# When the choices of experts are made between the gathered rows: shorter steps, other units, later copies

## What is computed

```python
def peer(h, p):
    n = h.shape[0]
    q = (h @ p['peer_wq']).reshape(n, PEER_HEADS, 2, PEER_HALF)
    s = jnp.einsum('nhcd,chkd->nhck', q, p['peer_keys'], preferred_element_type=F32)
    s1, i1 = lax.top_k(s[:, :, 0], PEER_TOPK)
    s2, i2 = lax.top_k(s[:, :, 1], PEER_TOPK)
    cand_s = (s1[..., :, None] + s2[..., None, :]).reshape(n, PEER_HEADS, PEER_TOPK * PEER_TOPK)
    cand_i = (i1[..., :, None] * PEER_N_KEYS + i2[..., None, :]).reshape(n, PEER_HEADS, PEER_TOPK * PEER_TOPK)
    top_s, pos = lax.top_k(cand_s, PEER_TOPK)
    eidx = jnp.take_along_axis(cand_i, pos, axis=-1)
    g = jax.nn.softmax(top_s, axis=-1)
    act = jax.nn.gelu(jnp.einsum('nd,nhkd->nhk', h, p['peer_u'][eidx], preferred_element_type=F32))
    return jnp.einsum('nhk,nhkd->nd', (g * act).astype(h.dtype), p['peer_v'][eidx])
```

## Time and profile before

| | us |
|---|---|
| median of 3 runs | 1500.54 (1499.4 to 1501.41) |
| the profiled execution, its own time | 1503.75 |
| span of that execution, first to last instruction | 1502.1 |
| first gather of the experts, from the span's start | 791.95 |
| last dot | 1494.1 |

### The profile page before, as it was taken

One profiled execution on the slowest core, in us unless ns is written; L12 is line 12 of the kernel. 1 busy time (PEld: TensorE's weight loads), 2 busy tenths in 40 slices (PEclk: granted clock), 3 DMA queues, 4 the chain that ended last, 5 costly groups with the idle time before them and its releaser, 6 DMA issues. The chain is left out here.

```text
span 1502.1 us, 17250 instructions
## 1 busy us (share of the span) xinstructions
PE 1253.6 (83%) x4972; PEld 773.6 (52%) x4972; DVE 868.0 (58%) x2346; ACT 582.1 (39%) x1551; POOL 421.0 (28%) x504
## 2 busy tenths in 40 slices
PE   5998899998776977789989988877887776788786
PEld 4886588776654655578867544322332222232231
DVE  1044379997282436651135876889756895454443
ACT  1162238878373324500014443433343332343333
POOL 1320012222021300000003434434543486343331
PEclk8999899999698987989999999999999999999999
DMA  4462133324387720154139999999999987999997
GB/s 157 169 218 99 43 114 119 105 99 137 141 295 259 249 75 1 40 199 182 57 126 371 420 376 371 384 420 421 421 422 421 421 362 307 421 420 422 421 421 314
DMA packets 77881, 391.26 MB, mean 260 GB/s; under 512 B 13176, under 2 KB 22936, under 8 KB 40416
## 3 DMA queue, kind: packets, MB, share of 16 engines
q0 software_dynamic: 43104, 287.92, 47.1%
q1 hardware_dynamic: 33712, 100.68, 18.8%
q10 hardware_dynamic: 976, 1.61, 0.3%
HBM read 378.43 MB, written 11.60 MB: 260 GB/s over the span
## 5 line engine op out<-in xcount | busy, mean ns | idle before, releaser
L1963 DVE CUSTOM_DVE_ANT_0 pe_uv<-pe_uv,pe_hnat 128x1024 f32<-128x1024 f32 x264 | 321.7, 1220 | 183.5 <-DMA pe_uv<-d_uv,pe_idx 169.7
L1832 POOL DMA_INDIRECT pe_uv<-d_uv,pe_idx x256 | 309.4, 1209 | 375.5 <-PE pe_acc L1711 182.4
L1711 PE MATMUL pe_ph<-pe_uv,pe_dg 128*128 128x512 f32 x512 | 256.4, 627 | 76.7 <-ACT pe_dg L1778 76.6
L1711 PE MATMUL pe_acc<-pe_uv,pe_dg 128*128 128x512 f32 (+1 forms) x544 | 260.7, 619 | 55.6 <-ACT pe_dg L1778 55.4
L181 PE MATMUL pi_ps<-xn,pi_w 128*128 128x264 f32 x944 | 225.0, 395 | 9.5 <-PEq L87 9.5
L1711 PEld LDWEIGHTS pe_ph<-pe_uv,pe_dg 128*128 128x128 f32 x512 | 89.1, 192 | 243.4 <-ACT pe_dg L1778 176.7
L1711 PEld LDWEIGHTS pe_acc<-pe_uv,pe_dg 128*128 128x128 f32 (+1 forms) x544 | 96.7, 189 | 211.2 <-ACT pe_dg L1778 120.3
L181 PEld LDWEIGHTS pi_ps<-xn,pi_w 128*128 128x128 f32 x944 | 181.1, 195 | 41.6 <-issue 11.4
L1772 ACT ACTIVATE pe_gl<-pe_a 128x1 f32<-128x1 f32 x264 | 53.0, 201 | 345.7 <-DVE pe_a L1963 345.6
L1778 ACT ACTIVATE pe_dg<-cst,pe_w 128x128 f32<-128x128 f32 x256 | 102.7, 401 | 8.3
L1775 ACT ACTIVATE pe_w<-pe_gl,pe_gw 128x1 f32<-128x1 f32 x256 | 75.4, 295 | 8.3
(11 more groups left out here) (290 smaller groups left out, 1704.9 us busy)
## 6 DMA issues: line engine op xcount, KB each, us to landing
pi_w<-d_w_in SPq DMA_DIRECT2D x71, 512.0 KB, 3.5
mg_w<-d_w_ab SPq DMA_DIRECT2D x8, 1536.0 KB, 6.5
ss_h<-d_state SPq DMA_DIRECT2D x8, 1024.0 KB, 6.4
o_ssm_s<-ss_h SPq DMA_DIRECT2D x8, 1024.0 KB, 7.8
pq_w<-d_wq SPq DMA_DIRECT2D x16, 512.0 KB, 7.9
paged<-d_ck POOLq DMA_DIRECT2D x40, 128.0 KB, 3.3
lg_w<-d_w_in SPq DMA_DIRECT2D x10, 512.0 KB, 6.4
paged<-d_cv POOLq DMA_DIRECT2D x32, 128.0 KB, 4.8
```

The lines of the kernel that those rows point to most:

```text
L1711: mm = pe.matmul(accs[n][0:m, 4 * half:4 * half + 4, :], lhsT, uv[:, r, D_MODEL + half * 512:D_MODEL + (half + 1) * 512], start=False, sto ...
L1832: pool.indirect_dma_start(uv[:, r, :], None, k.d_uv[:], bass.IndirectOffsetOnAxis(ap=src, axis=0)).then_inc(gathered[r], 16)
L1963: dve.tensor_tensor_reduce(uv[:, r, 0:D_MODEL], uv[:, r, 0:D_MODEL], hnat[:, n, :], 1.0, 0.0, ALU.mult, ALU.add, a[:, r:r + 1]).then_inc(d ...
```

## The change

- `SPANS`: a stretch now gives the first unit and the unit at which the choice must be ready: (0, 7), (8, 22), (28, 44), (48, 64), (66, 116) and (128, 236), where they ended at 8, 24, 40, 56, 112 and 192.
- `STEPS` in place of `PACE`: the samples' choice makes one step each second unit.
- The long instructions of the comparison, multiplication and sum are cut to 4 heads each, so a choice of 8 heads has 12 of 1024 columns in place of 6 of 2048. Choices of 1 or 2 heads keep theirs, and the sums of L1899 stay whole.
- `LAG`: `weights` comes three units after `ready`. ScalarE's `exponents` comes behind the `weigh` of unit `ready`, and its wait for `chosen` stands at the first unit that uses the choice (`FIRST_USE`).
- TensorE's scores come four units after the second query, and ScalarE copies queries and scores two units after TensorE's unit.

```diff
-        SPANS = ((0, RING), (RING, 3 * RING), (3 * RING, 5 * RING), (5 * RING, 7 * RING), (7 * RING, 14 * RING),
-                 (PER, PER + 8 * RING))
-        PACE = (2, 1, 1, 1, 1, 1)
+        SPANS = ((0, 7), (8, 22), (28, 44), (48, 64), (66, 116), (PER, 2 * PER - 20))
+        STEPS = (2, 1, 1, 1, 1, 0.5)
+        LAG = 3
+        FIRST_USE = [tile * PER + h0 * TOPK for tile, h0, _ in CHOICES]
...
-        scores_at = {u + 2: n // 2 for u, n in query_at.items() if n % 2}
+        scores_at = {u + 4: n // 2 for u, n in query_at.items() if n % 2}
...
                 for i in range(LOOPS[n] * RING):
-                    for c, (first, end) in enumerate(SPANS):
-                        if BEFORE[n] + i == end:
+                    at = BEFORE[n] + i
+                    if at in FIRST_USE[1:-1]:
+                        act.wait_ge(chosen, FIRST_USE.index(at) + 1)
+                    weigh(n, i)
+                    for c, (first, ready) in enumerate(SPANS):
+                        if at == ready:
                             exponents(c + 1)
-                            act.wait_ge(chosen, c + 2)
-                    weigh(n, i)
-                    if n == 0 and i in query_at:
-                        query(query_at[i])
-                    if n == 0 and i in scores_at:
-                        scores(scores_at[i])
+                    if n == 0 and i - 2 in query_at:
+                        query(query_at[i - 2])
+                    if n == 0 and i - 2 in scores_at:
+                        scores(scores_at[i - 2])
...
+                parts = [(a, min(a + 4, H)) for a in range(0, H, 4)]
                 for which, (f, e) in enumerate(((fa, e1), (fb, e2))):
                     settled()
-                    one(dve.tensor_tensor(eq[0:m, at], f[0:m, at].unsqueeze(2).broadcast_to([m, N, TOPK]),
-                                          k.iota[0:m].unsqueeze(1).broadcast_to([m, N, TOPK]), ALU.is_equal))
-                    yield
+                    for a, b in parts:
+                        to = slice((h0 + a) * TOPK, (h0 + b) * TOPK)
+                        one(dve.tensor_tensor(eq[0:m, to],
+                                              f[0:m, to].unsqueeze(2).broadcast_to([m, (b - a) * TOPK, TOPK]),
+                                              k.iota[0:m].unsqueeze(1).broadcast_to([m, (b - a) * TOPK, TOPK]),
+                                              ALU.is_equal))
+                        yield
...
-                    for c, (first, end) in enumerate(SPANS):
-                        if at == end:
+                    for c, (first, ready) in enumerate(SPANS):
+                        if at == ready:
                             for _ in rest:
                                 pass
+                        if at == ready + LAG:
                             weights(c + 1)
                         if at == first:
                             rest = choose(c + 1)
                     dot(n, i)
-                    for c, (first, end) in enumerate(SPANS):
-                        if first <= at < end:
-                            for _ in range(PACE[c]):
+                    for c, (first, ready) in enumerate(SPANS):
+                        if first <= at < ready:
+                            for _ in range(int((at - first + 1) * STEPS[c]) - int((at - first) * STEPS[c])):
                                 next(rest, None)
```

More of the change, by code:

```diff
@@ L1921, in choose @@
                 i4 = idf[0:m, 2 * h0:2 * h1].rearrange("p (h c) i -> p h c i", c=2)
+                parts = [(a, min(a + 4, H)) for a in range(0, H, 4)]
                 for which, (f, e) in enumerate(((fa, e1), (fb, e2))):
                     settled()
-                    one(dve.tensor_tensor(eq[0:m, at], f[0:m, at].unsqueeze(2).broadcast_to([m, N, TOPK]),
-                                          k.iota[0:m].unsqueeze(1).broadcast_to([m, N, TOPK]), ALU.is_equal))
-                    yield
-                    settled()
[L1928 to L1931, removed]
+                    for a, b in parts:
[5 more added lines that the diff above has]
+                        yield
+                    settled()
+                    for a, b in parts:
+                        to = slice((h0 + a) * TOPK, (h0 + b) * TOPK)
+                        e4 = eq[0:m, to].rearrange("p (h i) j -> p h i j", h=b - a)
+                        one(dve.tensor_tensor(e4, e4, i4[:, a:b, which, :].unsqueeze(2)
+                                              .broadcast_to([m, b - a, TOPK, TOPK]), ALU.mult))
+                        yield
                     settled()
-                    one(dve.tensor_reduce(e[0:m, at], eq[0:m, at], AX.X, ALU.add))
-                    yield
+                    for a, b in parts:
+                        to = slice((h0 + a) * TOPK, (h0 + b) * TOPK)
+                        one(dve.tensor_reduce(e[0:m, to], eq[0:m, to], AX.X, ALU.add))
+                        yield
                 settled()
```

## The result

The changed kernel takes **1480.34 us** in the median of four runs (1476.51 to 1481.99), the kernel before 1500.97 us (1499.4 to 1502.4) in runs beside it. The ratio is **0.9855, 95% interval 0.9835 to 0.9874**: some 21 us faster. 1478.0 us was predicted, with a range from 1473.5 to 1490.5.

What follows compares the result with a forecast made beforehand. The prediction took the experts to be bound by DMA at 421 GB/s, with two holes to fill. Terms of 10 and 12.5 us off the median of 1500.54 gave 1478.0 us, range 1473.5 to 1490.5.

Steps and rivals of the forecast that it cites:

- What bounds the kernel: Experts, from 792 us: DMA at 421 GB/s is the bound, except in holes at 870 to 990 and 1230 to 1270 us.
- First term: Prompt's part, 870 to 990 us: late weights and late copies fill the DMA hole, 10 us, ends 0 and 11.8.
- the chain at unit 24: ScalarE waits 5.97 us for a query, VectorE 9.25 for exponents, TensorE idles 4.51; unit 32's gather goes 7 us late.
- The deduction of 1.5 us for TensorE: Units 24 to 42: TensorE needs 25.7 us per ten units against DMA's 24.9, so it falls back 1.5 us.
- Second term: Samples' choice, 1230 to 1270 us: breaking VectorE's unbroken row ends the 20.07 us gather, 12.5 us, ends 0 and 15.5.
- The rule against it: Skill page on VectorE and GpSimd's shared ports: the lock lasts one instruction, so an unbroken row would not explain 20.07 us.
- The rival built on it: Samples' choice: the long gather has another cause and comes back, 1490.5 us, chance 0.07.
- Tile 1's choice, zero: Units 66 to 116: 44 steps in 50 units, the cut ones fitting their units; extra instructions hidden beside DMA, zero cost.
- The shut-out: Rival in tile 1's choice: 12 cut steps without a pause hold GpSimd, 20.6 us lost, 1498.6 us, chance 0.04.
- The samples' lists, zero: Lists come 47 units later; their 15.1 us through DRAM is hidden in 22.4 us, with 7 us to spare, zero cost.
- The sum, 22.5 us: Whole kernel: 10 and 12.5 us off the median of 1500.54 give 1478.0 us, chance 0.77.
- What was to show it: Signs: 415 GB/s from 1190 us, weights waiting under 1 us, no long TensorE idle, last dot near 1472 us.

Runs made afterwards that it cites:

- e1_prompt_part: The changed kernel with the samples' choice put back as before, so only the prompt's part is left; 1491.19 us, ratio 0.9934.
- e5: The changed kernel with ScalarE's query and score copies back at the queries' own unit, exponents and weights still late; 1480.73 us, ratio 0.9880.
- e6: The changed kernel with exponents, ScalarE's wait and weights at one unit again, copies still late; 1480.42 us, ratio 0.9865.
- e12: The changed kernel with the prompt's old spans and copies at once, only exponents and weights late, samples' choice still changed; 1484.61 us, ratio 0.9886.
- e10: The changed kernel with late copies and late weights both undone, so the prompt's part keeps only the new spans; 1488.45 us, ratio 0.9914.
- e9: The changed kernel with eight places for query weights in place of four, weights loaded four queries earlier; 1480.09 us, ratio 0.9861.
- e4: The changed kernel with the samples' steps uncut, still one step each second unit; 1480.54 us, ratio 0.9866.
- e3: The changed kernel with the samples' choice at one step each unit, steps still cut in two; 1482.53 us, ratio 0.9876.
- e7: The kernel before with the samples' choice run on all 128 partitions in place of 8; 1488.41 us, ratio 0.9929.
- e2: The kernel before with only the samples' choice changed: steps cut, one each second unit; 1489.35 us, ratio 0.9920.

## Why the prediction was right, step by step

- **What bounds the kernel.** Right. With both holes filled the experts run at DMA's pace, 420 to 422 GB/s in every stretch from 790 to 1390 us.
- **First term, 10 us with ends 0 and 11.8.** Measured 171.0 - 160.5 = 10.5 us from unit 8 to unit 70 (10.7 in e1_prompt_part). The mechanism was half told. I followed the chain at unit 24 and let both delays take part; e5 and e6 show that, at the new spans, either alone does it, and e12 that a second wait stands behind the chain at unit 40, for scores, which the new spans remove. The new spans, which I gave no price of their own, bring 2.1 us alone (e10). The deduction of 1.5 us for TensorE was right in kind: in the changed kernel it doesn't pause from 805.82 to 925 us, and e9 shows it as the bound as soon as there is less to transfer.
- **Second term, 12.5 us with ends 0 and 15.5.** Measured 195.6 - 184.0 = 11.6 us from unit 130 to unit 202. The size was right: the hole itself was 12.4 us, and one more late landing of another kind (last section) takes 1.0 of them back. The cause was too wide. "VectorE's unbroken row" was the observation, and a row is one of three conditions. The rest that I counted on is enough by itself (e4); that the cut steps are, too (e3), I did not foresee. The estimate of at most 4.6 us for a hold was kept: 3.32.
- **The rule against it.** The Trainium skill, "SBUF — State Buffer", section "SBUF: two separate sides", has the lock between VectorE and GpSimd held for one whole instruction, by VectorE in a two-port mode or with two inputs in SBUF. With 128 partitions the trace agrees (e7): 3.05 us beside a step of 2.29 with two inputs, 0.94 beside a sum, which has one. With 8 partitions it disagrees: 20.07 us over six steps, two of them sums, and the dots between, and in e4 no passage between a step and the dot behind it. The rival built on it fell with e1, e2 and e4.
- **Tile 1's choice, zero.** The shut-out didn't move there: gathers beside the cut steps take 1.97 to 2.00 us. The piece 70 to 130 is 1.8 us longer than before, as it is in e1_prompt_part, whose steps in it are whole; so the cut is not the reason. The last section has it: late landings beside loads of code, three in place of one.
- **The samples' lists, zero.** SyncE starts them from 1404.29 to 1410.31 us, and the piece from 202 to the end is 162.1 us long, as in e3 (161.8), whose choice ends long before.
- **The sum, 22.5 us.** The medians moved by 20.6, the ratio says 21.8. In the experts of the two profiles it is 19.6: 10.5 + 11.6 and 0.4 ahead of unit 8, less 1.8 and 1.1 in the two other pieces. The late landings of the last section are the term that I did not have.
- **What was to show it.** VectorE's waits and TensorE's idle time went as said. One stretch, 1390 to 1430 us, has 410 GB/s and not 415. The last dot starts at 1466.86 us and not near 1472: the 7.5 us ahead of the experts again.

## What to carry to other kernels

Where DMA sets the pace, look for the stretches in which it is not full, follow the late transfer to the engine that waits, and put a few units of distance into that chain; here one break in it was enough, and the second is cover. Where a gather on GpSimd is held beside VectorE, any of a pause, a shorter instruction or more partitions may free it, so try the cheapest. And compare two kernels by landings inside the stage that was changed: here one profile of each was off by 7.5 us for reasons ahead of it.

## What the runs showed of the hardware

**Few partitions hold a gather.** A whole step of 8 x 2048 and one of 128 x 2048 take the same 2.3 us, yet in an unbroken row GpSimd gets through at the end of the second and not of the first.

**Beside loads of program code, gathers land a microsecond late.** Units land 2.484 us apart in the median of the pieces 70 to 130 and 130 to 202 of the changed kernel, but eight of them (73, 86, 103, 133, 136, 155, 177 and 201) land 3.4 to 3.5 us behind the one ahead; outside these pieces units 54 and 240 do too. On VectorE's timeline such a unit is unit 54, whose dot waits 1.62 us where the one ahead waits 0.19:

```profile
933.47 1.23 DVE L1975 CUSTOM_DVE_ANT_0 pe_uv<-pe_uv,pe_hnat 128x1024 f32<-128x1024 f32 x1 [0.19 <-DMA pe_uv<-d_uv,pe_idx]
...
936.93 1.22 DVE L1975 CUSTOM_DVE_ANT_0 pe_uv<-pe_uv,pe_hnat 128x1024 f32<-128x1024 f32 x1 [1.62 <-DMA pe_uv<-d_uv,pe_idx]
```

Two of the page's DMA queues carry instructions:

```profile
q8 instruction: 39, 0.64, 0.2%
q14 instruction: 50, 0.41, 0.1%
```

In the packet records, the late landings of units 54, 73, 86, 136, 155, 177, 201 and 240 come 2.06 to 2.10 us behind the start of an 8 KB packet of code on queue 14, and that of unit 103 comes 2.99 behind one. The packet takes 0.31 to 0.33 us, and 0.31 to 0.32 us behind its start a gather's packet begins that takes 0.97 us where the median is 0.31: 0.32 + 0.66, or 1.0 us. In each trace the sixteen parts of a gather's landing, one from each DMA engine, have times of their own. The last part came 0.08 us behind the last but one at unit 53; it came 1.06 behind at unit 54, 2.04 at 73, 2.69 at 86, 3.69 at 103, and 6.54 at 240. So one engine falls some 1.0 us further behind each time, and the unit is complete when that one is done. Units 54, 73, 86, 103, 136, 155, 177 and 201 are late in e4_whole_second_unit too, whose times lie some 4 us later, so it goes with the place in the program. About every second packet of queue 14 has the slow packet behind it; why the others don't, no run shows. Nor did a run take the loads away, so that the code is the cause is argued from nine late landings out of nine.

Unit 133 is of another kind: ScalarE issues the store of tile 0's 512 KB of output at 1129.47 us, 1.25 us at 421 GB/s, and unit 133 is late in all fourteen traces.

This accounts for the pieces. For the 72 units from 130 to 202, 72 x 2.484 = 178.8 us; the store takes some 1.2 and four late landings 1.0 each, and the changed kernel takes 184.0. From 70 to 130 it is 60 x 2.483 = 149.0 and three late ones, 152.1 in all. The kernel before has one late one there (150.3), and the store, three late ones and the hole of the samples' choice from 130 to 202: 195.6 - 72 x 2.486 - 1.2 - 3 x 1.0 = 12.4 us for the hole itself. Some of the loads that cost the changed kernel a microsecond passed in the kernel before without one. There the engine that had fallen behind caught up in a hole: its part came 3.88 us behind the last but one at unit 166, and at unit 167, behind the hole, the last two lie 0.02 apart.

The Trainium skill, "Runtime: NRT & Kernel Launch", section "Instruction fetch mechanics", calls the cost of crossing a 16 KiB boundary of code mostly hidden. For the 16 KB packets of queue 8 the trace agrees: no unit lands a microsecond late by one of them alone, for example behind those at 1062.84, 1215.14 and 1295.49 us. Beside the 8 KB packets of queue 14, on a stretch that DMA bounds, the transfers land later.
